# Transformer trunk with a product-key expert layer: the first weight loads cut into pieces, the mixer steps one or two slots earlier, and TensorE's expert product moved next to its dot

## What is computed

```python
def peer_ffn(h, w_q, sub_keys, u_tab, v_tab):
    q = (xt @ w_q).reshape(T, PEER_HEADS, 2, PEER_HALF)
    s = jnp.einsum('thpd,hpkd->thpk', q, sub_keys).astype(F32)
    s_top, i_top = lax.top_k(s, PEER_TOPK)
    cand = (s_top[:, :, 0, :, None] + s_top[:, :, 1, None, :]).reshape(T, PEER_HEADS, -1)
...
    best, pos = lax.top_k(cand, PEER_TOPK)
    idx = jnp.take_along_axis(cand_idx, pos, axis=-1)
    gates = jax.nn.softmax(best, axis=-1)
...
        act = jnp.einsum('chkd,cd->chk', u_tab[ib], xb)
        act = (jax.nn.gelu(act.astype(F32)) * gb).astype(xb.dtype)
        return jnp.einsum('chk,chkd->cd', act, v_tab[ib])

    for i in range(DEPTH):
...
        hn = rmsnorm(h, norm_mix[i])
        if m == 0:
            y = diff_attention(hn, attn_w_qkv[j], attn_q_gain[j], attn_k_gain[j],
...
        elif m == 1:
            y = short_conv(hn, conv_w_in[j], conv_w[j], conv_w_out[j])
...
        h = h + y
        h = h + peer_ffn(rmsnorm(h, norm_ffn[i]), peer_w_q[i], peer_keys[i], peer_u[i], peer_v[i])
```

## Time and profile before

| | |
|---|---|
| median of 3 runs | 1543.76 us (1542.81 to 1544.13) |
| profiled execution | 1543.85 us, of which span 1541.7 us |
| granted TensorE clock, mean | 0.986 |
| busy: PE, DVE, ACT, POOL | 1352.9, 1005.3, 595.9, 587.5 us |
| moved by DMA | 623.92 MB, mean 405 GB/s |

### The profile page before, as it was taken

The page is one execution under the profiler, slowest core; times in us unless marked ns, Lnnn a source line. Parts: engine busy times, 40 slices in busy tenths (PEclk is TensorE's granted clock), DMA queues, the critical chain, the costliest instruction groups (busy, mean ns, idle before and its releaser), DMA issues.

```text
span 1541.7 us, 12630 instructions
## 1 busy us (share of the span) xinstructions
PE 1352.9 (88%) x3294; PEld 574.4 (37%) x3294; DVE 1005.3 (65%) x2481; ACT 595.9 (39%) x1805; POOL 587.5 (38%) x516
## 2 busy tenths in 40 slices
PE   8899899899868989889887899898979889778787
PEld 3454344344323433334332334343433333222222
DVE  5677878786567867446478635676657867755454
ACT  1324364544333434334334423243434344343333
POOL 0024243344323434335435433333434444344441
PEclk9999999999999999999999999999999999999999
DMA  9659999999999999999999999999999999999996
GB/s 394 247 215 421 421 421 422 421 389 421 421 423 421 416 421 421 421 421 422 421 421 418 422 422 421 416 418 421 405 421 366 422 421 421 421 421 421 422 421 289
DMA packets 85319, 623.92 MB, mean 405 GB/s; under 512 B 9472, under 2 KB 9600, under 8 KB 11648
## 3 DMA queue, kind: packets, MB, share of 16 engines
q0 software_dynamic: 73728, 536.90, 84.3%
q1 hardware_dynamic: 9792, 78.91, 12.4%
q10 hardware_dynamic: 1728, 7.31, 1.2%
HBM read 622.04 MB, written 1.05 MB: 404 GB/s over the span
## 4 chain that ended last, share of the span: by engine, by line
DMA 43%; PE 35%; DVE 11%; ACT 7%; issue 3%; POOL 0%; SPq 0%; ACTq 0%; DVEq 0%; POOLq 0%
DMA ring<-in_peer_uv_dram,idx 42%; PE acc L607 23%; PE pp L364 10%; DVE ring L1379 6%; ACT diag L928 1%; ACT L922 1%; ACT weight L924 1%; PE acc L364 1%; DMA ring<-in_w_qkv_dram 1%; ACT L784 1%; PE tt L379 1%; ACT gelu L922 1%; ACT work L747 1%; PE ss L438 0%; DVE row_f L1145 0%
## 5 line engine op out<-in xcount | busy, mean ns | idle before, releaser
L607 PE MATMUL acc<-ring,diag 128*128 128x512 f32 x2048 | 997.4, 613 | 174.2 <-ACT diag L928 169.5
L705 POOL DMA_INDIRECT ring<-in_peer_uv_dram,idx x512 | 587.3, 1147 | 933.5 <-PE acc L607 816.8
L1379 DVE CUSTOM_DVE_ANT_0 ring<-ring,xf 128x1024 f32<-128x1024 f32 x512 | 627.0, 1226 | 461.4 <-DMA ring<-in_peer_uv_dram,idx 451.5
L607 PEld LDWEIGHTS acc<-ring,diag 128*128 128x128 f32 x2048 | 371.5, 192 | 736.0 <-ACT diag L928 389.5
L922 ACT ACTIVATE gelu<-dots 128x1 f32<-128x1 f32 x512 | 103.6, 202 | 804.5 <-DVE dots L1379 804.1
L928 ACT ACTIVATE diag<-const,weight 128x128 f32<-128x128 f32 x512 | 205.5, 401 | 16.7
L924 ACT ACTIVATE weight<-gelu,gates 128x1 f32<-128x1 f32 x512 | 150.8, 295 | 16.6
L364 PE MATMUL pp<-stream,xT 128*128 128x512 f32 x160 | 81.5, 599 | 0.0
L364 PE MATMUL pp<-stream,rows 128*128 128x512 f32 x128 | 66.3, 599 | 0.0
L364 PEld LDWEIGHTS pp<-stream,xT 128*128 128x128 f32 x160 | 30.3, 192 | 37.1 <-issue 37.1
L1379 DVE DVE_READ_ACCUMULATOR2_ANT dots<- 128x1 f32 x512 | 42.3, 83 | 0.0
(11 more groups left out here) (150 smaller groups left out, 742.6 us busy)
## 6 DMA issues: line engine op xcount, KB each, us to landing
stream<-in_peer_w_q_dram SPq DMA_DIRECT2D x18, 1024.0 KB, 9.3
stream<-in_conv_w_in_dram SPq DMA_DIRECT2D x16, 1024.0 KB, 9.7
stream<-in_w_qkv_dram SPq DMA_DIRECT2D x8, 1024.0 KB, 9.4
ring<-in_peer_uv_dram,idx POOLq DMA_INDIRECT x512, 15.3
ring<-in_w_qkv_dram SPq DMA_DIRECT2D x3, 2048.0 KB, 24.6
stream<-in_w_o_dram SPq DMA_DIRECT2D x4, 1024.0 KB, 17.2
kept<-in_peer_w_q_dram SPq DMA_DIRECT2D x2, 2048.0 KB, 11.6
kept<-in_w_qkv_dram SPq DMA_DIRECT2D x1, 2048.0 KB, 36.5
```

The source lines that it names most:

```text
L607: mm = nc.tensor.matmul(acc[half][:, :], diag[:, s % RING, :], row[:, D + half * 512:D + (half + 1) * 512], start=(k == 0), stop=(k == SLO ...
L705: nc.gpsimd.indirect_dma_start(dst, None, uv_dram, bass.IndirectOffsetOnAxis(idx[:, at:at + 1], 0)).then_inc(landed, 16)
L1379: nc.vector.tensor_tensor_reduce(row[:, 0:D], row[:, 0:D], xf[:, s // SLOTS % 2, :], 1.0, 0.0, ALU.mult, ALU.add, dots[:, s % RING:s % RIN ...
```

## The change

- **Loads of the front.** The last 1.5 MiB of the first chunk now come as three pieces of 512 KB (`w_first_in[2]`, `w_first_in[3]`, `w_in[4]`), the second chunk as two halves of 1 MiB (`w_second_in`, `w_in[5]`), and PE waits for the piece that a matmul reads. ACT issues the load of `h[:, 0, :]` when the piece `w_first_in[3]` has landed; before, when the first piece `w_first_in[0]` had.
- **Products.** PE's loop is now `if s > 0: add_expert(s - 1)`, then the sides of slot s.
- **Table.** Window 1's steps stand one slot earlier, windows 2 and 3's two slots. Window 1's `out00` and `out10` go from 68 and 72 to 60 and 65, `wq2` from 120 to 112 and `wq3` from 134 to 120, while their rankings stand at 133 and 149 (`RANK_AT`; before 133 and 147). Window 0's chunk 3 is projected one slot earlier and ranked at 66 in place of 63.
- **Ranking.** Window 3's chunk 0 is ranked in one step a slot, no longer two.
- In windows 2 and 3 PE waits for each half of the turned input by itself.

```diff
--- before.py
+++ after.py
@@ -62,24 +62,25 @@
 
 AT = (
     {},
-    dict(q0=12, k0=22, q1=30, k1=54,
-         logits0=25, bias0=26, max0=30, exp0=31, diff0=35, turn0=38, values0=42,
-         logits1=57, bias1=58, max1=62, exp1=63, diff1=68, turn1=71, values1=75,
-         norm0=45, norm1=77, gain=54, y0=49, y1=81, out00=68, out10=72, out01=84, out11=88, h0=87, f0=89, h1=91, f1=93, scale=92,
-         wq0=93, wq1=104, wq2=120, wq3=134),
-    dict(x=3, in2=8, in4=16, in3=24, in5=32, in0=40, in1=48, z0=25, z1=41, turn_z0=27, turn_z1=43, turn_g0=51, turn_g1=59,
-         conv0=30, conv1=46, gain=20, times0=54, times1=61, out00=62, out10=66, out01=70, out11=74, h0=74, f0=76, h1=78, f1=80,
-         scale=79, wq0=84, wq1=98, wq2=152, wq3=176),
-    dict(x=3, in2=8, in4=16, in3=32, in5=40, in0=56, in1=64, z0=25, z1=49, turn_z0=27, turn_z1=51, turn_g0=67, turn_g1=75,
-         conv0=30, conv1=54, gain=20, times0=69, times1=77, out00=71, out10=75, out01=79, out11=83, h0=83, f0=85, h1=87, f1=89,
-         scale=88, wq0=89, wq1=106, wq2=132, wq3=156),
+    dict(q0=12, k0=21, q1=29, k1=53,
+         logits0=24, bias0=25, max0=29, exp0=30, diff0=34, turn0=37, values0=41,
+         logits1=56, bias1=57, max1=61, exp1=62, diff1=67, turn1=70, values1=74,
+         norm0=44, norm1=76, gain=54, y0=48, y1=80, out00=60, out10=65, out01=83, out11=87, h0=86, f0=88, h1=90, f1=92, scale=91,
+         wq0=92, wq1=104, wq2=112, wq3=120),
+    dict(x=2, in2=6, in4=14, in3=22, in5=30, in0=38, in1=46, z0=23, z1=39, turn_z0=25, turn_z1=41, turn_g0=49, turn_g1=57,
+         conv0=28, conv1=44, gain=20, times0=52, times1=59, out00=60, out10=64, out01=68, out11=72, h0=72, f0=74, h1=76, f1=78,
+         scale=77, wq0=82, wq1=96, wq2=150, wq3=174),
+    dict(x=2, in2=6, in4=14, in3=30, in5=38, in0=54, in1=62, z0=23, z1=47, turn_z0=25, turn_z1=49, turn_g0=65, turn_g1=73,
+         conv0=28, conv1=52, gain=20, times0=67, times1=75, out00=69, out10=73, out01=77, out11=81, h0=81, f0=83, h1=85, f1=87,
+         scale=86, wq0=87, wq1=106, wq2=132, wq3=156),
 )
 SECOND_HEAD = 0
 FIRST_NORM = 8
-LATE_RANK_PROJECT = {1: 0, 2: 25, 3: 50}
+LATE_RANK_PROJECT = {1: 0, 2: 24, 3: 49}
+RANK_AT = {(0, 3): 66, (1, 2): 133, (1, 3): 149}
 HALF = KT // 2
-RANK_PIECES = {(0, 1): 2, (0, 2): 2, (0, 3): 1, (1, 0): 2, (3, 0): 2}
-LATE_IN_PROJECT = {2: 9, 1: 17, 5: 33, 3: 41}
+RANK_PIECES = {(0, 1): 2, (0, 2): 2, (0, 3): 1, (1, 0): 2}
+LATE_IN_PROJECT = {2: 8, 1: 16, 5: 32, 3: 40}
 SHARED = {(1, "in", 0), (1, "in", 4), (1, "in", 5), (1, "out", 0), (1, "wq", 3),
           (3, "in", 2), (3, "in", 3), (3, "out", 0), (3, "out", 1), (3, "wq", 2), (3, "wq", 3)}
 PARTS = 2
@@ -91,6 +92,18 @@
 def pieces(n, c):
 
     return RANK_PIECES.get((n, c), 1)
+
+
+def ranked_at(n, c):
+
+    if (n, c) in RANK_AT:
+        return RANK_AT[n, c]
+    return 13 + (steady_of(n)[f"wq{c}"] if n else LATE_RANK_PROJECT[c])
+
+
+def after_project(n, c):
+
+    return (9, 12, 13, 15, 16) if (n, c) == (0, 3) else (8, 10, 10, 12, 12)
 
 
 def gates_from(n, c):
...
@@ -348,6 +362,11 @@
                 if place == STREAM:
                     if k % DEEP == 0:
                         pe.wait_ge(part_in[k // DEEP], 16 * (before + 1))
+                elif (n, what, c) == (0, "in", 2):
+                    if k == 0:
+                        pe.wait_ge(w_second_in, 16)
+                    elif k == HALF:
+                        pe.wait_ge(w_in[place], 16)
                 elif k == 0:
                     pe.wait_ge(w_in[place], 16 * (before + 1))
 
@@ -452,6 +471,8 @@
                         pe.wait_ge(w_first_in[k], 16)
                     if k == 4:
                         pe.wait_ge(x_scaled, 2)
+                        pe.wait_ge(w_first_in[3], 16)
+                    if k == 6:
                         pe.wait_ge(w_in[4], 16)
                     mm = nc.tensor.matmul(bank[:, :], xT[:, k, :], by_row[:, k, :], start=(k == 0), stop=(k == KT - 1))
                 mm.then_inc(pp.written_sem((0, "in", 0)), 1)
@@ -520,9 +541,10 @@
                         yield from project(pp, n, "wq", c, xT, at + HALF * half, range(HALF * half, HALF * (half + 1)))
                 else:
                     yield from project(pp, n, "wq", c, xT, at)
-                yield at + 10
+                _, turn, _, score_at, _ = after_project(n, c)
+                yield at + turn
                 turn_queries(n, c)
-                yield at + 12
+                yield at + score_at
                 score_keys(n, c)
 
             def late(c):
@@ -578,10 +600,11 @@
                     yield at["x"] + c
                     turn_h(n, "x", c)
                 for i, c in enumerate(in_order(n)):
-                    yield at[f"in{c}"]
-                    if i == 0:
-                        copied(pe, tt, (n, "x", 0), (n, "x", 1))
-                    yield from project(pp, n, "in", c, xTm, at[f"in{c}"])
+                    for half in range(2):
+                        yield at[f"in{c}"] + HALF * half
+                        if i == 0:
+                            copied(pe, tt, (n, "x", half))
+                        yield from project(pp, n, "in", c, xTm, at[f"in{c}"] + HALF * half, range(HALF * half, HALF * (half + 1)))
 
             def turn_gated(n):
                 at = steady_of(n)
@@ -617,10 +640,9 @@
             for n in (2, 3):
                 sides += begun(gated_input(n), turn_gated(n), output(n), turn_output(n), *(experts(n, c) for c in range(4)))
             for s in range(ALL):
-                if s > 1:
-                    add_expert(s - 2)
+                if s > 0:
+                    add_expert(s - 1)
                 along(sides, s)
-            add_expert(ALL - 2)
             add_expert(ALL - 1)
 
 
@@ -643,7 +665,11 @@
                     sp.dma_start(place[:, k * CHUNK:(k + 1) * CHUNK], columns[:, k * CHUNK:(k + 1) * CHUNK]).then_inc(w_first_in[k], 16)
                 sp.dma_start(xT[:, 4:KT, :].rearrange("p k t -> p (k t)"), x_cols[0][:, 4 * P:]).then_inc(x_cols_in[0], 16)
                 sp.dma_start(place[:, 2 * CHUNK:4 * CHUNK], columns[:, 2 * CHUNK:4 * CHUNK]).then_inc(w_first_in[2], 16)
-                sp.dma_start(place[:, 4 * CHUNK:], columns[:, 4 * CHUNK:]).then_inc(w_in[4], 16)
+                sp.dma_start(place[:, 4 * CHUNK:6 * CHUNK], columns[:, 4 * CHUNK:6 * CHUNK]).then_inc(w_first_in[3], 16)
+                sp.dma_start(place[:, 6 * CHUNK:], columns[:, 6 * CHUNK:]).then_inc(w_in[4], 16)
+                place, columns = places[held(0, "in", 2)[0]], matrix_of(0, "in", 2)
+                sp.dma_start(place[:, 0:4 * CHUNK], columns[:, 0:4 * CHUNK]).then_inc(w_second_in, 16)
+                sp.dma_start(place[:, 4 * CHUNK:], columns[:, 4 * CHUNK:]).then_inc(w_in[5], 16)
 
             def load_stream(n, what, c, before, previous):
 
...
@@ -785,7 +811,7 @@
 
             def front():
                 act.dma_start(const[:, :], consts).then_inc(const_in, 16)
-                act.wait_ge(w_first_in[0], 16)
+                act.wait_ge(w_first_in[3], 16)
                 act.dma_start(h[:, 0, :], x_rows[0]).then_inc(x_in[0], 16)
                 act.wait_ge(w_in[5], 16)
                 act.dma_start(bias[:, :, :], bias_rows).then_inc(bias_in, 16)
@@ -827,14 +853,15 @@
                 exponential_gates(0, 0, range(0, 1))
                 copy_in(ff, 1, 4)
 
-            def rank(n, c, at, rank_at):
-                yield at + 8
+            def rank(n, c, at):
+                queries, _, turned, _, scores = after_project(n, c)
+                yield at + queries
                 copy_queries(n, c)
-                yield at + 10
+                yield at + turned
                 copy_turned(n, c)
-                yield at + 12
+                yield at + scores
                 copy_scores(n, c)
-                yield rank_at + gates_from(n, c)
+                yield ranked_at(n, c) + gates_from(n, c)
                 exponential_gates(n, c)
 
             def second_head():
...
@@ -1307,7 +1333,7 @@
                 expert_rows(n)
 
             def experts(n, c):
-                at = steady_of(n)[f"wq{c}"] + 13
+                at = ranked_at(n, c)
                 yield at
                 yield from paced(ranked(n, c), at, pieces(n, c))
                 yield at + gates_from(n, c) + 1
```

12 lines of the change are left out of this document (6 added, 6 removed).

## The result

The changed kernel takes 1546.93 us (median of 15 runs, 1545.85 to 1548.59) against 1543.11 us (15 runs, 1542.51 to 1545.68): ratio 1.0020, 95% interval 1.0014 to 1.0027. The medians differ by 3.8 us, and the ratio is worth 3.1. The forecast was 1543.0, no change within 3.1 us, with a range of 1537.5 to 1548.5; the time lies within the range, but the kernel is slower, clear of the noise.

What follows compares the result with a forecast made beforehand. Prediction: gathers bound the kernel at 421 GB/s, the engines' front chain before them. From 1543.85: front +5.5, window 3's ranking -4.5, window 1's pile -1.5, earlier `wq2`/`wq3` -0.3 gave 1543.05, forecast 1543.0 us; range 1537.5 to 1548.5.

Steps and rivals of the forecast that it cites:

- Full rate, 421 GB/s; the front bounds until the first gather: Whole kernel: gathers bound at 421 GB/s, taken as full; before the first gather the engines' front chain bounds, losing 34.0 us.
- A dip is worth its missing bytes: Middle stretches: time is lost wherever DMA's mean rate is under 421 GB/s; dips priced at 3.0 and 4.8 us.
- window 3's ranking: At 1150 to 1210 us: ranking chunk 0 over 16 slots closes the dip, -4.5 us (bounds -3 and -4.8).
- the reserve: Steady part: queued gathers let an engine be about 5 us late at no cost.
- Pieces, 0 to -0.3: Front: loading the first chunks in pieces gains PE 3.5 us, but is worth only 0 to 0.3 us in time.
- `h`, +3.8: Front: `h` issued 4.7 us later and landing after 9.4 us delays DVE; less 0.9 us back, +3.8 us.
- TensorE's clock, +2.2 and -0.5: Front: a new PE pause around 27 to 35 us lowers its clock, +2.2; the old pause's cost at 58 us shrinks, -0.5.
- Window 1's pile, -1.5: At 290 to 350 us: moved work frees DVE and PE, winning half of the 3.0 us dip, -1.5 (0 to -3).
- The rest, 0 with bounds 0 and +3: PE's product one slot behind: waits each under one slot, taken up by 5 us of reserve, 0 us (bounds 0 and +3).
- products and sides hold each other: Slower rival: ACT and DVE wait for PE steps behind a product waiting for them; 1548 to 1550 us, chance 0.08.
- The pile moves, it doesn't go: Slower rival: dips give back only 1.5 us while the front costs 5.5 to 6; 1548.0 us, chance 0.14.
- the dips' gain of 6.3 us: Windows 1 and 3: gains expected from window 3's ranking (-4.5), window 1's pile (-1.5) and earlier `wq2`, `wq3` (-0.3).

Runs made afterwards that it cites:

- b_pieces_copy: Kernel before with the front in pieces, `h` early, and ScalarE's first copy ahead of its wait for the second chunk and five transfer issues: 1541.45 us, ratio 0.9987.
- b_rank16: Kernel before with one edit, window 3's chunk 0 ranked in one step a slot (16 slots, not 8): 1543.09 us, ratio 0.9997.
- b_busy68: Kernel before with 9.8 us of extra, unused VectorE work added at slots 68 to 71: 1546.91 us, ratio 1.0022.
- a_old_chunks: Changed kernel with window 1's out00, out10, wq2, wq3 and the selection places put back as before: 1545.73 us, ratio 1.0014.
- a_old_front_two: Changed kernel with the old front and the product two slots behind, so only mixers and chunks moved: 1543.39 us, ratio 1.0001 to the kernel before.
- a_two_behind: Changed kernel with TensorE's expert product again two slots behind the slot's dot: 1544.93 us, ratio 1.0010 to the kernel before.

## Why the forecast was wrong, step by step

- **Full rate, 421 GB/s; the front bounds until the first gather.** Held: 420 GB/s at 1210 to 1510 us, and a first gather 1.5 us sooner in b_pieces_copy goes with a span 1.2 us shorter (1540.5).
- **A dip is worth its missing bytes.** This is the step that failed most. It gave window 3's ranking -4.5; the dip shrank, and the term is 0 (b_rank16 0.9997). What it missed is that the reserve differs from share to share. Of the gathers issued at 1140 to 1160 us the first share lands 7.3 and the last 15.0 us after the issue, and at slot 0, with nothing queued, it is 5.2 and 5.8. So the fastest engine has about 2 us queued there and the slowest about 9 (estimates from these four times), and 5.5 us of lateness empty the one and not the other. At 306 to 330 us the last share lands after 9.3 us, a reserve of 3.5, and there the added work cost time (b_busy68).
- **Pieces, 0 to -0.3.** TensorE's times were right: the first chunk without a pause to 14.0, the second chunk at 13.87. Their value was wrong: 0.0017, or 2.6 us lost (1.7 by the sum of the halves), and where these are lost stays open. I named VectorE's row at 30.83 as what TensorE would wait for, and did not ask what held VectorE at 21.45. The earlier trace rows has the answer, ScalarE's copy at 20.75; what stood ahead of it was in the trace, and I took only the table load of it into the count. That explains why nothing was won.
- **`h`, +3.8.** The issue was right (9.86 against 9.8), the landing 1.6 us too late in my count (7.7 us, not 9.4), and ScalarE's queue covered part of the rest: +2.1 at VectorE's first square, +1.07 at the first gather, nothing in the medians. Bare, it is 2.8 us at 62 us and 3.9 at the first gather, clock included.
- **TensorE's clock, +2.2 and -0.5.** The pause of 4 to 8 us did not come. There was one wait of 2.47 us, with the lower clock from 23.5 to 26.9 us, and behind 64.5 us only 3.4 us of it instead of the 6.8 at the earlier trace rows. The first cost nothing, since VectorE is 2.1 us behind ahead of it and behind it; the second gave back 1.0 us. The sign of the second term was right, its size too small.
- **Window 1's pile, -1.5.** 399 GB/s at 290 to 350 us, as before (400), and the moved chunks cost 0.9 us by a_old_chunks (0.0006, within the noise). With the product two behind the rate did rise there (411 in a_old_front_two, 415 in a_two_behind) and fell to 379 to 401 from 360 to 380 us, where the kernel before has 420 and 421: the pile moved. I had seen the pile and not the two additions behind it.
- **The rest, 0 with bounds 0 and +3.** The product one behind costs 1.0 to 1.5 us (0.0007 to 0.0010), within the bounds and each just inside the noise. My reason has the engines the wrong way round: VectorE waits in order for TensorE, for 10.6 us in two places and not for under a slot each. That the reserve takes it up holds for the product alone; but the chunks use the same reserve, and I gave each term the whole of it.
- **Mixers sooner**, which had no term of their own, win about 1 us (0.9993, an interval that just includes no change).

Of the rivals, "products and sides hold each other" (0.08) comes closest behind the front, with VectorE waiting for steps that stand behind a product; it was priced 1 to 3 us too high. "The pile moves, it doesn't go" (0.14) gave 1548.0 and is right that window 1's dips remain. By the parts, the loss is front, product and chunks, less what the mixers win. That the time lies within the range is in part luck: the front was priced some 3.5 us too high and the dips' gain of 6.3 us did not come, and the two errors partly cancel.

## What to carry to other kernels

Ask of an engine that is to be sped up not who waits for it, but what every engine on that path is doing at that moment, its queue of transfer issues and table loads included: a front in pieces took 2.6 us more than the kernel before, and 2.0 us less once one copy was moved ahead of five issues (1.0017 and 0.9987). Price a dip in a transfer-bound stretch by the latest share of a transfer, not by the mean rate; early in a stream the two are nearly the same, late they are not. Before a step is moved on one engine, look for in-order waits of another engine on the steps behind it, above all where buffers come free behind them, and count the reserve once for all edits that draw on it.

## What the hardware showed that I had not expected

- The sixteen shares of a gather drift apart as the stream goes on, 0.7 us at its start and mostly 8 to 10 us at slots 290 to 350, and a dip brings them together again (3.9 us behind the dip at slot 384). 262 GB/s for 20 us cost only 1.3 us.
- The transfer of `h` took 9.4 us from issue to landing at 5.1 us and 7.7 us at 9.9 us, behind the same queue of weights.
- The same code reached its first gather between 95.50 and 98.22 us in four different executions, with TensorE's lower clock at other places between 60 and 80 us in each, so one trace can't measure an edit of 1 us in the front.
